# Delta rule levels: the two banks of R and Z read crosswise by vector and scalar engine

## The reference, cut to what matters

```python
kk = jnp.einsum("bhncd,bhnjd->bhncj", k, k)
L = jnp.where(strict, beta[..., :, None] * kk * decay, 0.0)
rhs = jnp.concatenate([beta[..., None] * v, (beta * jnp.exp(G))[..., None] * k], axis=-1)
sol = lax.linalg.triangular_solve(jnp.eye(CHUNK, dtype=f32) + L, rhs, left_side=True,
                                  lower=True, unit_diagonal=True)
```

## Time and profile before

| | |
|---|---|
| median of 3 runs | 2180.52 us (2180.33 to 2181.97) |
| the profiled execution | 2182.54 us |
| its span | 2180.7 us |
| PE busy | 99% of the span |
| DVE, ACT, POOL busy | 59%, 48%, 21% |
| granted clock of PE, mean | 0.998 |

### The profile page before, as it was taken

One profiled execution on the slowest core, in us unless ns is written; L12 is line 12 of the kernel. 1 busy time (PEld: TensorE's weight loads), 2 busy tenths in 40 slices (PEclk: granted clock), 3 DMA queues, 4 the chain that ended last, 5 costly groups with the idle time before them and its releaser, 6 DMA issues.

```text
span 2180.7 us, 33607 instructions
## 1 busy us (share of the span) xinstructions
PE 2152.2 (99%) x12460; PEld 1767.8 (81%) x12460; DVE 1284.8 (59%) x2333; ACT 1037.7 (48%) x1950; POOL 468.3 (21%) x372
## 2 busy tenths in 40 slices
PE   9999999999999999999999999999999999999998
PEld 7777778888888888877777787777788888889887
DVE  5545665445845546577787524666556457757464
ACT  6555654333534435455756533544435445434244
POOL 2443320001201102354554550000010001101001
PEclk9999999999999999999999999999999999999999
DMA  5223212333333323322122234232233413323333
GB/s 180 80 69 104 66 59 78 101 93 93 101 93 106 96 88 107 98 78 88 59 74 59 59 92 126 80 86 78 78 96 120 123 59 98 101 92 107 97 101 93
DMA packets 107218, 199.31 MB, mean 91 GB/s; under 512 B 11800, under 2 KB 13976, under 8 KB 106800
## 3 DMA queue, kind: packets, MB, share of 16 engines
q1 hardware_dynamic: 107056, 197.16, 29.8%
HBM read 194.97 MB, written 2.15 MB: 90 GB/s over the span
## 4 chain that ended last, share of the span: by engine, by line
PE 94%; DVE 2%; ACT 2%; issue 1%; DMA 0%; SPq 0%; POOL 0%; DVEq 0%; ACTq 0%; POOLq 0%
PE bank L1258 24%; PE bank L1264 24%; PE bank L1260 24%; PE bank L1210 19%; PE bank L1213 3%; PE bank L1279 1%; PE bank L1282 1%; PE bank L1284 1%; DVE ya L2276 0%; ACT L2097 0%; DMA x<-in_xT 0%; ACT whi L1787 0%; DVE fout L2276 0%; ACT sbA L1969 0%; DVE gv L2279 0%
## 5 line engine op out<-in xcount | busy, mean ns | idle before, releaser
L1787 ACT ACTIVATE whi<-stage 128x512 fp32r<-128x512 f32 x668 | 413.9, 626 | 414.1 <-PE bank L1264 356.4
L1258 PE MATMUL bank<-hh,whi 128*128 128x512 f32 x1456 | 585.8, 402 | 0.0
L1264 PE MATMUL bank<-hh,wlo 128*128 128x512 f32 x1456 | 568.8, 391 | 0.4 <-DVE wlo L2276 0.4
L1260 PE MATMUL bank<-hl,whi 128*128 128x512 f32 x1456 | 567.7, 390 | 0.1
L2276 DVE TENSOR_TENSOR wlo<-stage,whi 128x512 fp32r<-128x512 f32 x492 | 378.7, 786 | 63.8 <-ACT whi L1787 59.2
L1264 PEld LDWEIGHTS bank<-hh,wlo 128*128 128x128 f32 x1456 | 273.2, 188 | 60.6 <-DVE wlo L2276 1.5
L1258 PEld LDWEIGHTS bank<-hh,whi 128*128 128x128 f32 x1456 | 273.9, 188 | 55.7 <-issue 2.8
L1260 PEld LDWEIGHTS bank<-hl,whi 128*128 128x128 f32 x1456 | 274.1, 188 | 54.4 <-issue 1.2
L2866 POOL TENSOR_TENSOR wlo<-stage,whi 128x512 fp32r<-128x512 f32 x176 | 239.3, 1367 | 300.4 <-ACT whi L1787 300.2
L2276 DVE TENSOR_TENSOR x<-bank,x 128x512 f32<-128x512 f32 (+1 forms) x81 | 55.5, 685 | 170.3 <-PE bank L1264 170.2
L2866 POOL TENSOR_TENSOR acc<-acc,sqb 128x512 f32<-128x512 f32 x34 | 45.7, 1345 | 278.5 <-ACT sqb L1800 278.5
(11 more groups left out here) (442 smaller groups left out, 4024.1 us busy)
## 6 DMA issues: line engine op xcount, KB each, us to landing
stage<-in_wall SPq DMA_DIRECT2D x682, 256.0 KB, 2.7
gbc<-rows SPq DMA_DIRECT2D x8, 512.0 KB, 4.2
band<-in_toep SPq DMA_DIRECT2D x16, 256.0 KB, 3.4
x<-in_xT SPq DMA_DIRECT2D x8, 256.0 KB, 6.1
fb<-rowsf SPq DMA_DIRECT2D x8, 256.0 KB, 3.6
out_y<-fout SPq DMA_DIRECT2D x8, 256.0 KB, 2.6
memx<-in_memT SPq DMA_DIRECT2D x1, 1024.0 KB, 9.3
memx<-in_mem2T SPq DMA_DIRECT2D x1, 1024.0 KB, 4.8
```

The source lines that it names most:

```text
L1258: pe.matmul(o, wh, hi, start=j == 0, stop=False)
L1260: pe.matmul(o, wh, lo, start=False, stop=False)
L1264: i = pe.matmul(o, wl, hi, start=False, stop=end)
L1787: act.activation(k.whi[u % NSPLIT][:], k.source(u), ACT.Copy).then_inc(*up("whi", u))
```

## The change

In levels 0 to 4 P and Z are made in two halves. DVE first takes the R columns of bank 3, while ACT copies the Z columns of bank 4; then DVE waits for ACT's first half and takes the R columns of bank 4, and ACT waits for DVE's first half and copies the Z columns of bank 3. ACT's first half waits for `pe_lz` and no longer for P. E is made as before, of all 256 columns, after both halves of P. PE's waits are the same. The order of the steps is not changed.

```diff
     def prep_level(h, n, u):          # ACT
         if n < 5:
-            act.wait_ge(*at("gp_P", (h, n + 1)))
-            act.activation(k.gL.rearrange("p (k c) -> p k c", k=2), halves[:, :, 0:256], ACT.Copy).then_inc(*up("gp_Z", (h, n + 1)))
+            act.wait_ge(*at("pe_lz", (h, n)))
+            act.activation(k.gL[:, 256:512], bank[4][:, 0:256], ACT.Copy).then_inc(*up("gp_Zodd", (h, n + 1)))
+            act.wait_ge(*at("gp_Peven", (h, n + 1)))
+            act.activation(k.gL[:, 0:256], bank[3][:, 0:256], ACT.Copy).then_inc(*up("gp_Z", (h, n + 1)))
...
     def prep_level(h, n, u):          # DVE
         if n < 5:
             dve.wait_ge(*at("pe_lz", (h, n)))
-            lev = k.cf("lev", 64 * (n + 1), 64).unsqueeze(1).unsqueeze(1).to_broadcast([128, 2, 2, 64])
+            lev = k.cf("lev", 64 * (n + 1), 64).unsqueeze(1).to_broadcast([128, 2, 64])
             P = k.gM[:, 0:256]
-            tt(blocks4(P), halves[:, :, 256:384].rearrange("p k (b c) -> p k b c", c=64), lev, ALU.mult).then_inc(*up("gp_P", (h, n + 1)))
+            tt(c4(P[:, 0:128]), c4(bank[3][:, 256:384]), lev, ALU.mult).then_inc(*up("gp_Peven", (h, n + 1)))
+            dve.wait_ge(*at("gp_Zodd", (h, n + 1)))
+            tt(c4(P[:, 128:256]), c4(bank[4][:, 256:384]), lev, ALU.mult).then_inc(*up("gp_P", (h, n + 1)))
             dve.wait_ge(*at("gp_P", (h, n + 1)))
             tt(c4(k.gE[:, 0:256]), const4("eye"), c4(P), ALU.subtract).then_inc(*up("gp_E", (h, n + 1)))
```

More of the change, by code:

```diff
@@ L2674, in prep_kk @@
         tt(k.gL, bank[4], k.gD, ALU.mult).then_inc(*up("gp_lt", h))
-    def blocks4(t):
-        return t.rearrange("p (k b c) -> p k b c", k=2, b=2)
     def eye4(r):
```

## The result

The changed kernel takes 2199.76 us (2199.43 to 2200.24, 4 runs) and the kernel before 2180.74 (4 runs): 19.0 us more, ratio 1.0084 with a 95% interval of 1.0072 to 1.0096. The forecast was 2197.0 in a range of 2191.5 to 2201.0.

What follows compares the result with a forecast made beforehand. The prediction took PE to bound the kernel (busy 2152.2 of 2180.7 us). Stalls of 10.3 + 1.68 + 0.59 + 0.59 = 13.2 us plus 3.3 for PE's clock gave 16.5, so 2197.0 us, range 2191.5 to 2201.0.

Steps and rivals of the forecast that it cites:

- PE bounds, and the added wait on DVE is what matters: All hand-overs: PE's added waiting sets the time; DVE, mid-P, now waits for ACT's odd copy, with E and its queue behind.
- After level 3, 2.08 per head, heads 2 to 5: ACT copies late behind its table load, so cuu is late and PE starts 2.08 us later per head.
- After level 4, 0.50: Heads 2 to 5: E comes last, delaying PE's last level by 0.50 us per head on top of 2.08.
- Head 6, 0.59; head 0, 0.59: Head 6 after level 3 and head 0 after level 4: PE waits for the later E, 0.59 us each.
- Head 1, 1.68: After level 3, with ACT at Z at 996.31, PE's cpt,cuu comes 1.68 us later; nothing added after level 4.
- After level 0, 0: E is held until the POOL operation in progress ends, so starting 0.29 us later costs 0.
- My bound of 0.3 for each of heads 0 and 1: After level 0, by plain addition of E's later start where PE followed closely: some 0.3 us per head.
- The clock, 3.3 us by falls in three of four heads: Heads 2 to 5: longer waits lower PE's clock, 1.1 us net per fall, three falls taken, 3.3 us; ends 0 and 4.4.
- The first: Rival: same stalls but PE's clock holds; 13.2 us more, 2193.7; chance 0.25.
- The second: Rival: DVE stall absorbed, only last-level hand-overs cost; 3.2 us more, 2183.7; chance 0.05.
- third: Rival: faster, ACT free 0.3 to 0.4 sooner, carried to gv; up to 2.6 us gained, 2177.9; chance 0.02.
- the fourth: Rival: displaced DVE operations stretch beside POOL's, or heads 0 to 6 all have clock falls; 10 us more, 2207; chance 0.06.

Runs made afterwards that it cites:

- e4: Changed kernel with the same halves not crosswise: DVE never waits for ACT, ACT copies each bank after DVE's half; 2181.28 against 2180.58 us, ratio 1.0003.
- e6: Changed kernel; after level 3 of heads 1 to 5 DVE does values and cuu before waiting for ACT, then odd half and E; 2189.43 us, 1.0034 of before.
- e5: Changed kernel plus nine unread PE products in front of PE's wait for cuu after level 3, heads 2 to 5; 2196.92 against 2181.81 us, ratio 1.0068.
- e3: Crosswise halves only after levels 0, 1 and 2, elsewhere the code of the kernel before; 2181.44 us, +0.9, ratio 1.0005.
- e1: Crosswise halves only after level 3, elsewhere the code of the kernel before; 2194.61 against 2180.58 us, +14.0, ratio 1.0065.
- e8: Changed kernel with the old form (whole P, whole Z) after level 0, crosswise after levels 1 to 4; 2197.48 against 2181.88 us, ratio 1.0069.
- e10: Kernel before, unread PE products in head 0 behind level 5's bank waits and behind level 5, cuu ahead of values in heads 1 to 5; 2182.00 us, 1.0001.
- e2: Crosswise halves only after level 4, elsewhere the code of the kernel before; 2184.52 us, +3.9, ratio 1.0019.

## Why the prediction was right, and where it was not

- *PE bounds, and the added wait on DVE is what matters.* Right: e4, without the crossing, has no loss that can be told from none, and e6, which only moves what stood behind the wait ahead of it, has 11 us less of the 19.
- *After level 3, 2.08 per head, heads 2 to 5.* Right: the waits of 2.69 are the 0.60 of before and 2.09. After level 4, 0.50: PE waited 0.46 to 0.50 for E in e5. Per head 2.59 to 2.64 against 2.58.
- *Head 6, 0.59; head 0, 0.59.* Right: 0.62 and 0.59. *Head 1, 1.68*: it was 1.2. ACT came to its copy at 994.90, 1.41 ahead of the 996.31 of the earlier trace rows, while PE was 1.06 ahead; I had taken the copy's start as fixed.
- *After level 0, 0.* Wrong. That E is held to the end of a POOL operation in progress was read rightly in head 3: in e3 it starts 0.29 later there, takes 1.01 in place of 1.30, and PE loses nothing. I carried this to all heads without looking at each. In heads 2 and 7 E met the start of the next operation, and PE lost 0.65 and 0.68 there, 1.3 in all. In the changed kernel heads 5 and 6 lose 0.29 and 0.16 at this place too, and heads 3 and 4 win 0.38 and 0.35; none of these four is in e3, so they belong to what the falls of the clock displace. My bound of 0.3 for each of heads 0 and 1 was on the wrong heads and too small.
- *The Trainium skill on the ports* (SBUF — State Buffer, section "Who interferes with whom"): the mechanism is as it says, one of VectorE and GpSimd is blocked for a whole instruction of the other. What follows from it, and what I overlooked, is that some 0.3 us of delay can cost 0.65 or nothing, by which operation is met. The traces have both.
- *The clock, 3.3 us by falls in three of four heads.* This is the term that was most wrong. The falls came in all four, twice as long in two of them, and cost 3.9 by the medians and 4.9 by the level starts; and the longer low stretch in head 0 (1.3 by the level starts) was missed. The term was right in kind and too small by 2 to 3. A wait of 2.69 is not enough by itself for a fall: of the twelve in the profiles of the changed kernel, e1 and e8 ten were followed by one, and head 5 of e1 and head 4 of e8 were not. What decides it is not shown. The Trainium skill's account (TensorE: Matmul & The Clock Gate, section "HAM oscillation — how this bites in real kernels") has the kind of thing, a fall again in each round with a gap; its example has longer waits than these, and here ten rounds of twelve agree. A fall doesn't cost the same each time: from level 3 of one head to the next PE lost 2.97 and 2.94 in heads 2 and 3, only 0.35 more than in e5, because PE, when slow, no longer waits at level 5, but 4.55 and 4.90 in heads 4 and 5, where the clock was low for twice as long.
- *Rivals.* The first (the clock holds) had the stalls at 13.2. Without a clock term the level starts have 10.45 for heads 2 to 5, 1.2 for head 1, 0.62 and 0.59 for heads 6 and 0, together 12.9; so the stalls were as forecast and the clock was not as this rival had it. The second and third did not occur. Of the fourth, displaced DVE operations did stretch beside POOL's (E after level 0 of heads 2 and 7), at 1.3 us and not 10.

What was missed, by the level starts: 1.6 for the falls in heads 2 to 5 (4.9 and not 3.3), 1.3 for the clock in head 0, 1.3 after level 0 and 0.2 for stalls, less 0.5 that head 1 cost less and 0.5 that was given back. That is 3.4 of the 19.8 - 16.5 = 3.3 there; by the medians the forecast was short by 2.5. That the time lies inside the range is in part luck: the range's upper end had room for the falls (1.1 more) and level 0 (0.6) without either having its right size or place.

## What to carry to other kernels

A change that lets two engines take turns makes the first wait for the second, and the price isn't in the shortened instructions but in what stands in the first engine's queue behind that wait, at the place where the second engine is late (here behind a table load). Look for that place in the trace and follow the queue to what the bounding engine waits for. If the order has to be kept, move what others wait for ahead of the new wait, and then look at what this pushes back.

## What the hardware did that I had not expected

- The kernel before has two times on one chip: of its 21 executions beside e10, 8 lie from 2179.96 to 2180.84 and 13 from 2181.73 to 2182.98. The distance, 1.7 to 2, is that of one fall of PE's clock. In the profiled execution of before the clock fell near 100 us, in that of the changed kernel it did not, with the same wait of 1.98 in front:

```profile
100.00:104.00 4.00, 3.52 (x27) 2.13 (x28) 0.71 (x2) 1.82 (x4) 1.21 (x1) 1.00 0.18 64
```

  So the same wait lowers the clock in one execution and not in another. All 14 profiled executions run the same code up to head 0. From the row behind this wait to level 0 of head 0 it is 840.84 to 840.98 us in the five with the fall (before, e2, e5, e6, e10) and 839.15 to 839.29 in the nine without it: this fall costs 1.7 us, and no execution lies between the two groups. That it makes the two groups of times is likely; it isn't shown run by run, as the other executions have no profile.
- Nine products in each of four heads, 2.3 us a time, done for nothing, made the changed kernel some 3 to 4 us faster.
